# A two-block transformer on one core: the modulation dot products move to GpSimd, the third norm moves behind the projections, the first attention units run in pairs

## The reference

```
def memory_attention(q_mem, mem, mem_norm, w_mem_kv):      # first attention units: 4 heads of 64, 256 keys
    kv = rmsnorm(mem, mem_norm) @ w_mem_kv
    p = softmax(q k^T / 8);  o = p v

def first_block(x, mem, ...):
    ... layer a, layer b ...
    return rmsnorm(x, final_norm)

def _layer(x, c, ..., norm_g, w_ada, b_ada, w_in, ...):    # the third stage
    mod = c @ w_ada + b_ada                                # c: 1024 values, w_ada: 1024 x 3072
    shift, scale, gate = split(mod, 3)
    h = rmsnorm(x, norm_g) * (1 + scale) + shift
    proj = h @ w_in                                        # 1024 x 4096
    sb_q, sb_k, sb_v, sb_g, df_q, df_k, df_v, df_g = split(proj)
    ... stick-breaking attention (8 heads), differential attention (4 heads) ...
    return x + gate * (concat(sb_out, df_out) @ w_out)
```

## Time and profile before

| | us |
|---|---|
| median of 3 runs | 1594.12 (1592.28 to 1594.25) |
| profiled execution, its time | 1589.25 |
| its span | 1587.4 |
| TensorE busy | 1510.7 (95%) |
| VectorE busy | 931.4 (59%) |
| ScalarE busy | 671.4 (42%) |
| GpSimd busy | 110.5 (7%) |
| 24 loads of w_ada, issue to landing, median | 5.3 |

### The profile page before, as it was taken

The page is one execution under the profiler, slowest core; times in us unless marked ns, Lnnn a source line. Parts: engine busy times, 40 slices in busy tenths (PEclk is TensorE's granted clock), DMA queues, the critical chain, the costliest instruction groups (busy, mean ns, idle before and its releaser), DMA issues.

```text
span 1587.4 us, 20131 instructions
## 1 busy us (share of the span) xinstructions
PE 1510.7 (95%) x7120; PEld 1169.9 (74%) x7120; DVE 931.4 (59%) x1361; ACT 671.4 (42%) x1083; POOL 110.5 (7%) x127
## 2 busy tenths in 40 slices
PE   5988999999999999999989999999999799999998
PEld 4866677888888887766668888888887466667767
DVE  6668667777774335645445777777343644445662
ACT  6533344444443223434344444444222345555561
POOL 1269300000000000000000000000000010000000
PEclk9999999999999999999999999999999899999999
DMA  6544122223223222111112223223322111111221
GB/s 230 178 166 172 41 80 90 96 94 102 95 97 109 92 86 80 54 54 54 49 44 94 93 94 105 92 92 112 104 92 76 62 54 53 55 64 56 67 93 53
DMA packets 38146, 141.85 MB, mean 89 GB/s; under 512 B 4356, under 2 KB 4612, under 8 KB 38088
## 3 DMA queue, kind: packets, MB, share of 16 engines
q1 hardware_dynamic: 36936, 138.98, 25.8%
q10 hardware_dynamic: 1152, 2.10, 0.3%
HBM read 138.97 MB, written 2.10 MB: 89 GB/s over the span
## 4 chain that ended last, share of the span: by engine, by line
PE 83%; DVE 8%; ACT 5%; issue 2%; POOL 1%; DMA 1%; SPq 0%; ACTq 0%; DVEq 0%
PE ps L329 17%; PE ps L330 17%; PE ps L331 17%; PE ps L345 7%; PE ps L347 6%; PE ps L346 6%; DVE wl L263 2%; PE ps L510 2%; PE ps L580 1%; DVE rbc L426 1%; ACT wh L257 1%; PE ps L568 1%; PE ps L1796 1%; POOL aw L800 1%; PE ps L1786 1%
## 5 line engine op out<-in xcount | busy, mean ns | idle before, releaser
L257 ACT CAST wh<-raw 128x1024 fp32r<-128x1024 f32 (+1 forms) x213 | 234.0, 1099 | 312.1 <-PE ps L331 259.3
L263 DVE TENSOR_TENSOR wl<-raw,wh 128x1024 fp32r<-128x1024 f32 (+1 forms) x213 | 275.3, 1292 | 134.9 <-ACT wh L257 134.6
L329 PE MATMUL ps<-xh,wh 128*128 128x512 f32 x728 | 286.0, 393 | 9.7 <-DVE xl L1402 8.0
L330 PE MATMUL ps<-xl,wh 128*128 128x512 f32 x728 | 284.0, 390 | 0.0
L331 PE MATMUL ps<-xh,wl 128*128 128x512 f32 x728 | 283.9, 390 | 0.0
L345 PE MATMUL ps<-xh,wh 128*128 128x512 f32 x448 | 193.0, 431 | 2.5 <-DVE wl L263 2.5
L347 PE MATMUL ps<-xh,wl 128*128 128x512 f32 x448 | 177.8, 397 | 0.0
L346 PE MATMUL ps<-xl,wh 128*128 128x512 f32 x448 | 177.2, 396 | 0.0
L329 PEld LDWEIGHTS ps<-xh,wh 128*128 128x128 f32 x728 | 136.9, 188 | 43.6 <-issue 8.6
L331 PEld LDWEIGHTS ps<-xh,wl 128*128 128x128 f32 x728 | 137.1, 188 | 28.8
L330 PEld LDWEIGHTS ps<-xl,wh 128*128 128x128 f32 x728 | 137.1, 188 | 28.4 <-issue 0.5
(11 more groups left out here) (264 smaller groups left out, 2178.2 us busy)
## 6 DMA issues: line engine op xcount, KB each, us to landing
raw<-w_a_f SPq DMA_DIRECT2D x44, 512.0 KB, 3.2
raw<-w_b_f SPq DMA_DIRECT2D x44, 512.0 KB, 3.2
aw<-w_ada SPq DMA_DIRECT2D x24, 512.0 KB, 5.3
raw<-w_a_f SPq DMA_DIRECT2D x16, 704.0 KB, 4.1
raw<-w_b_f SPq DMA_DIRECT2D x16, 704.0 KB, 4.1
raw<-w_b_pair SPq DMA_DIRECT2D x18, 512.0 KB, 3.2
raw<-w_sb SPq DMA_DIRECT2D x16, 512.0 KB, 3.2
raw<-w_df SPq DMA_DIRECT2D x16, 512.0 KB, 3.2
```

The costliest lines, as they stand in the source:

```text
L257: nc.scalar.copy(wh[:, s, :width], raw[:, s, :width]).then_inc(w_hi, 1)
L263: nc.vector.tensor_tensor(wl[:, s, :width], raw[:, s, :width], wh[:, s, :width].bitcast(F32), ALU.subtract).then_inc(w_lo, 1)
L329: nc.tensor.matmul(dst, a, h(k), start=(k == 0), stop=False)
L330: nc.tensor.matmul(dst, a, l(k), start=False, stop=False)
```

## The change

1. The modulation no longer uses VectorE or TensorE. GpSimd loads, through its own queue, one tile of 128 rows of the transposed `w_ada` at a time (128x1024, 512 KB) into one buffer `rowt`, multiplies it by `vec`, a copy of `c_2` on every partition, and halves it ten times by additions until one column is left (`dot`). 24 such dots follow the first attention units. `vec` takes the place of the first layer's memory keys and values, so GpSimd waits for these units to be done.
2. After the 24 dots GpSimd forms `mod` and writes 8 diagonal tiles of the shift. Behind the `gate` chunk TensorE turns them with two matmuls into a copy of the shift on every partition, which ScalarE copies to `vec`. Then GpSimd makes 32 more dots, with the rows of `w_in_2` (another 16 MB from HBM): `csh`, what the shift adds to each column of each projection.
3. The third stage's projections run on x times gain and scale, which is split during `b_f2`. The norm's factor is applied when a projection leaves its bank, and for l = 0 to 2 a second instruction adds the column of `csh`; the gate's column goes in as the bias of its Silu. The first sum of squares goes to TensorE behind the first chunk of `sb`, the second behind the second.
4. The first layer's units run through `two_pe`, `two_act` and `two_dve`, which take their buffers as parameters.
5. SP's loads of `w_ada` are gone.

```diff
@@ gpsimd
-            for m in range(24):
-                a = aw[m % 6]
-                pool.wait_ge(ada_prod, m + 1)
-                for i, w in enumerate((4 * P, 2 * P, P)):
-                    wait(pool, ada_sum, 3 * m + i if i else 0)
-                    nc.gpsimd.tensor_tensor(a[:, 0:w], a[:, 0:w], a[:, w:2 * w], ALU.add).then_inc(ada_sum, 1)
+            def dot(i, rows, dst):
+                wait(pool, dot_sum, 11 * i)
+                pool.dma_start(rowt[:, :], rows).then_inc(row_in, 16)
+                pool.wait_ge(row_in, 16 * i + 16)
+                nc.gpsimd.tensor_tensor(rowt[:, :], rowt[:, :], vec[:, :], ALU.mult).then_inc(dot_sum, 1)
+                for e in range(10):
+                    w = 512 >> e
+                    pool.wait_ge(dot_sum, 11 * i + e + 1)
+                    nc.gpsimd.tensor_tensor(rowt[:, 0:w] if w > 1 else dst, rowt[:, 0:w], rowt[:, w:2 * w],
+                                            ALU.add).then_inc(dot_sum, 1)
+            pool.wait_ge(att["ma"]["pv"], 16)
+            pool.dma_start(vec[:, :], t["c_rep"]).then_inc(vec_in, 16)
+            pool.wait_ge(vec_in, 16)
+            for n in range(24):
+                dot(n, tile_rows("w_ada_rows", n), mod[:, n:n + 1])
...
+            for k in range(KD):
+                nc.gpsimd.tensor_scalar(rowt[:, k * P:(k + 1) * P], ident, mod[:, k:k + 1], None, ALU.mult).then_inc(diag, 1)
+            pool.wait_ge(rep, 2)
+            for n in range(32):
+                dot(24 + n, tile_rows("w_c_rows", n), csh[:, n:n + 1])
@@ vector, b_f2 and the third stage's start
                     nxt()
+                    x_lo_part(dve, X0["sb"], k, l // 2, modcol(8, k), xh, xl, square=False)
                     add_square(k, l // 2)
+            dve.wait_ge(ada_mod, 4)
             rounds(dve, "b_f2", 4, 4, split_lo, body)
-            norm_factor(dve, 5, rbc[:, :])
-            for k in range(KD + 1):
...
+            dve.wait_ge(dot_sum, 11 * 56)
+            q_shift = csh[:, 0:16].rearrange("p (u l) -> p u l", l=4)[:, :, 1:2]
+            nc.vector.tensor_scalar(q_shift, q_shift, QSCALE, None, ALU.mult).then_inc(k_cast, 1)
...
+                if n == C0["sb"]:
+                    split(u, l)
+                    norm_factor(dve, 5, rbc[:, :])
                 dve.wait_ge(w_used, n + 1)
...
-                    nc.vector.tensor_copy(dst, src).then_inc(po_free, 1)
-                if u == 0:
+                    nc.vector.tensor_tensor(dst, src, rbc[:, :], ALU.mult).then_inc(po_free, 1)
+                if l < 3:
+                    dve.wait_ge(po_free, J0["sb"] + 4 * u + l + 1)
+                    nc.vector.tensor_scalar(dst, dst, csh[:, 4 * u + l:4 * u + l + 1], None, ALU.add).then_inc(l_pr, 1)
@@ tensor
-            def ada(n):
-                pe.wait_ge(ada_sum, 3 * n + 3)
...
-                mem_att(att["ma"], u, "a", qma, pa, pta, (mix_lo, 1) if u else (m_vn, 4), between_a)
+                two_pe(pe, att["ma"], u, pa, pta, ..., (mix_lo, 1) if u else (m_vn, 4), between_a)
...
             norm_sum(pe, X0["kv"] + 8, 3)
+            pe.wait_ge(diag, KD)
+            for h in range(2):
+                nc.tensor.matmul(lg[h][:, :], ones, rowt[:, h * S:(h + 1) * S], start=True, stop=True).then_inc(rep_ps, 1)
...
             job(pe, [(C0["sb"], C0["sb"], KD)], J0["sb"], J0["sb"], X, XL, ready=(x_lo, X0["sb"]))
+            pe.wait_ge(n_hs, 24)
+            nc.tensor.matmul(st[:, :], ones, acc2[:, :], start=True, stop=True).then_inc(s_sum, 1)
+            blocks(pe, "sb", 1, X, XL, 0, KD)
             pe.wait_ge(s_root, 6)
             nc.tensor.matmul(st[:, :], ones, acc[:, :], start=True, stop=True).then_inc(s_sum, 1)
```

More of the change, by code:

```diff
@@ L104, in build @@
         cw = {L: par[:, NROWS + 176 * i:NROWS + 176 * (i + 1)].rearrange("p (a n) -> p a n", a=2) for i, L in enumerate("ab")}
-        km = {L: sb("km" + L, [P, 2, MEM], F32) for L in "ab"}
-        vm = {L: sb("vm" + L, [P, 2, MEM], F32) for L in "ab"}
+        vec_at = next_byte[0]
+        km, vm = {}, {}
+        for L in "ab":
+            km[L], vm[L] = sb("km" + L, [P, 2, MEM], F32), sb("vm" + L, [P, 2, MEM], F32)
+        vec = sb("vec", [P, D], F32, vec_at)
+        rowt = sb("rowt", [P, D], F32)
+        csh = sb("csh", [P, 32], F32)
         sm = sb("sm", [P, 64], F32)
@@ L427, in norm_factor @@
             dve.wait_ge(s_r, k + 1)
-        def att_pe(pe, a, it, q, k, v, nk, bias, first=None, o_free=None):
-            def turned(s):
-                h, i = divmod(s, TT)
-                n = nk(i)
-                pe.wait_ge(a["norm"], 8 * it + s + 1)
-                wait(pe, a["copy"], 8 * it + s - 1)
-                for b in range(n // P):
-                    mm = nc.tensor.transpose(tb[s % 2][:, b * P:(b + 1) * P],
-                                             first[:, s % 2, b * P:(b + 1) * P], ident)
-                mm.then_inc(a["turn"], 1)
-            def values(s, pt):
-                h, i = divmod(s, TT)
-                if s == 0 and o_free is not None:
-                    wait(pe, *o_free)
-                pe.wait_ge(a["copy"], 8 * it + s + 1)
-                for b in range(nk(i) // P):
-                    mm = nc.tensor.matmul(ob[heads(h), i * P:(i + 1) * P], v(h, b), pt[:, s % 2, b * P:(b + 1) * P],
-                                          start=(b == 0), stop=(b == nk(i) // P - 1))
-                mm.then_inc(a["pv"], 1)
-            def logits(s):
-                h, i = divmod(s, TT)
-                n = nk(i)
-                wait(pe, a["exp"], 8 * it + s - 1)
-                dst = lg[s % 2][:, :n]
-                more = bias(h, i, n)
-                mm = nc.tensor.matmul(dst, q(h, i), k(h, n), start=True, stop=not more)
-                for e, (c, l, r) in enumerate(more):
-                    mm = nc.tensor.matmul(lg[s % 2][:, c:n], l, r, start=False, stop=(e == len(more) - 1))
-                mm.then_inc(a["logit"], 1)
-            return logits, turned, values
@@ L585, in two_pe, with two_act @@
             pe_pairs(logits, turned, values, between)
[L587 removed]
+        def two_act(act, a, it, p, pt, nk, behind):
             def exps(s):
@@ new lines, in _ @@
+            pool.wait_ge(ada_mod, 1)
+            nc.gpsimd.tensor_scalar(mod[:, 8:16], mod[:, 8:16], 1.0, None, ALU.add).then_inc(ada_mod, 1)
+            for e, g in enumerate(("norm_g_2", "final_norm")):
+                pool.wait_ge(ada_mod, 2 + e)
+                nc.gpsimd.tensor_tensor(mod[:, 8:16], mod[:, 8:16], par[:, ROWS[g]:ROWS[g] + 8], ALU.mult).then_inc(ada_mod, 1)
+            for k in range(KD):
+                nc.gpsimd.tensor_scalar(rowt[:, k * P:(k + 1) * P], ident, mod[:, k:k + 1], None, ALU.mult).then_inc(diag, 1)
@@ L1711, in _ @@
             ffn("b", X0["b_f1"], 4)
-            pe.wait_ge(n_hs, 24)
-            nc.tensor.matmul(st[:, :], ones, acc2[:, :], start=True, stop=True).then_inc(s_sum, 1)
             def turn_values(u):
@@ L1930, in layout @@
     gate[:, 0:12] = kv[:, 2 * TOKW:2 * TOKW + 12]
-    heads4 = [chunk(w2, u + (4, 0, 8, 12)[l] + 16 * (u // 4) - 4 * (u // 4)) for u in range(8) for l in range(4)]
+    order4 = [u + (4, 0, 8, 12)[l] + 16 * (u // 4) - 4 * (u // 4) for u in range(8) for l in range(4)]
+    heads4 = [chunk(w2, c) for c in order4]
     out = {
@@ L1946, in layout @@
         "w_c_out": pack(*(chunk(a["w_out_2"][0], j) for j in range(KD))),
-        "w_ada": pack(*(chunk(a["w_ada_2"][0], n) for n in range(24))),
+        "w_ada_rows": pack(a["w_ada_2"][0].T),
+        "w_c_rows": pack(*(w2.T[c * P:(c + 1) * P] for c in order4)),
+        "c_rep": np.ascontiguousarray(np.broadcast_to(a["c_2"].reshape(1, D), (P, D))),
     }
```

176 lines of the change are left out of this document (49 added, 127 removed), and 2 rows, old and new, of the table PAR_ROWS.

## The result

The changed kernel is slower: 1616.24 us, median of 4 runs (1612.57 to 1618.31), against 1593.2 (1592.09 to 1594.25); the ratio is 1.0154 [1.0136, 1.0173]. The prediction was 1563 us with a range up to 1590 and a chance of 0.11 for slower: wrong in sign. The profiled execution took 1612.57 us, 23.3 more than that of before.

The account below looks back on a forecast made before the run. TensorE was taken to set the time nearly everywhere. Gains of 50.9 us less costs of 20.5 gave net −30.4: 1558.9 from the profiled 1589.25, plus 4.9 for the runs' median, said as 1563 us; range 1543 to 1590.

Parts of the forecast that it names:

- the feed-forward's term: Two first feed-forward halves: GpSimd's dots delay VectorE's weight splits through the shared port; cost 8 us, bounds 0 and 42.
- the clump: A dot's GpSimd product of 1024 columns and addition of 512 together, 2.4 + 1.3 = 3.7 us.
- B: Rival: VectorE becomes the bound beside the dots; 1587 us at worst, 1578 in the middle; chance 0.21.
- A: Rival: port conflicts between GpSimd and VectorE cost next to nothing, 3 to 8 us; time near 1548 us; chance 0.20.
- C: Rival: dots take 20 to 24 us and come late for `gate` and third stage; 1694 us; chance 0.11.
- the prediction's own signs of being wrong: First layer gains under 24 us, TensorE's `wl` waits in f1 sum over 20 us, or `ones` by `rowt` waits.
- Gain 1: Layer a's `a_in`: taking the modulation out brings the first unit's logits from 109.76 to 101.1 us; gain 8.7 us.
- Gain 2: First layer's two attention units run in pairs, as in layer b; gains 15.0 and 9.6 us.
- Gain 3: Third norm, last `b_f2` addition to transposes of first values: 23.2 us for 40.80; gain 17.6, between 14 and 18.
- One dot: GpSimd's load, product and additions for one dot take 14.7 us, load 4.2 of it; bounds 10.4 and 24.
- The small terms: Costs outside the feed-forward: spatial gating 3 us, layer b's attention 5, third stage's column additions 2.

Follow-up runs that it names:

- Run 5: Changed kernel, in first feed-forward halves a dot only every second round, its product held until the second tap of the first chunk ends: 1579.31 us, 0.9925.
- run 9: Changed kernel with a full dot only every fourth round of the first feed-forward halves, those between over one column (incomplete result): 1547.83 us, 0.9715.
- run 11: Changed kernel with dots on VectorE as one 1024-column operation, done twice in each round of the first feed-forward halves: 1566.91 us, 0.9857.
- Run 7: Changed kernel where GpSimd makes only each dot's product and ScalarE sums the row: 1601.12 us, 0.9994 to the kernel before is not this run; its ratio is 1.0056.
- run 1: Changed kernel with the dots' arithmetic cut to one one-column instruction, loads and waits kept (incomplete result): 1538.05 us, 0.9663.
- run 2: Changed kernel whose dots keep only the 1024-column product, the 512-column addition and the last one-column addition: 1591.07 us, 0.9993.
- run 10: Kernel before, with the modulation's VectorE products and GpSimd additions over one column, first units unpaired: 1572.43 us, 0.989.

## Why the prediction was wrong

**The step that failed** is the feed-forward's term: "The tightest split ends at 405.12, and TensorE wants it near 407.5 ...: 2.3 us of room. When the clump meets that place, 1.4 us are lost. ... I take it for a quarter of them, and some small change: 8 us. Bounds 0 and 30 × 1.4 = 42." Measured are 74.7, above the bound. The number of dots was right (31 of them start in the two halves); two things were wrong.

- *The room was taken for each dot anew.* 2.3 us is a stock, used up once; what a round puts back is 0.5 to 0.6 us (runs 5, 9 and 11). The earlier trace rows had half of it: VectorE waits 1.15 us for TensorE and then 0.40 for `wh`. Run 5's row has the other half: when VectorE comes 1.15 us earlier, it waits 1.04 for `wh`, so of the 1.15 only 1.15 − 0.64 = 0.51 are won there. I had read instead that VectorE was busy 7.95 of 10.88 us and called the rest free. With a dot in each round the loss is 3.16 − 0.61 = 2.55 (measured 2.6), not 3.7 − 2.3 = 1.4.
- *The places were taken as random.* In `a_f1` dot and round keep step at 13.5 us: the clump meets the split in 18 of its rounds, 17 of them running, and in 7 of `b_f1`, where the step was lost: 25 splits for 31 dots, not a quarter. That the two fall into step because each waits for the other is an inference from the timelines; no run shows it by itself. (Run 7 keeps step as well, by an explicit wait.) So an average over phases was no estimate here.

**The rivals.** B named the right engine, and its first sentence has "some 4.6 (GpSimd's held time) = 13.5 of 10.88 us", the very round of the trace. The size is luck: it adds 7.95 + 1 + 4.6, and the trace has 10.27 of cycle + 3.16 of delay; the gaps were put too low and the held time, for which no row stood, too high. I then charged 1.4 a dot from the other reasoning instead of 13.5 − 10.88 = 2.6, and so wrote 1587 "at worst". With 2.6 in 30 rounds the term is 78 instead of 8, and the forecast's sum −30.4 + 70 = +39.6: the right sign, 16 us above the traces' 23.4, since the halves lost 3 less than that and the other stretches did better by 13. A fell (runs 1 and 2). C fell: a dot took 11 to 15.6 us, no wait at `ones` by `rowt`. Of the prediction's own signs of being wrong one came: the waits for `wl` in the halves sum to 56 us, over the 20.

**Gain 1 and Gain 2.** The sum of 33.3 held (34.3, or 31.6 from the first chunk of `a_in` on). By place the parts held too: ahead of the units 8.1 from the first chunk on for the 8.7, in the units 23.5 (74.1 to 50.6 us) for 24.6. By cause they didn't. In the units the pairs alone bring 4.7 us, and 16.2 once the modulation is light (66.8 us in run 10 against 50.6, the modulation's steps on TensorE in it). The modulation's arithmetic alone brings 7.3 in the units. It stood in their way: of the 7.4 us of the earlier trace rows, 2.6 lay there, and I had put them all into `a_in`.

**Gain 3.** From the last addition to the first values 23.7 us pass now instead of 40.80: 17.1 for the forecast's 17.6, with a granted clock of 1.00 for 0.83. The other 2.3 us of the table's 19.4 lie ahead of it: the rounds of `b_f2` take 15.11 us instead of 15.40, at a granted clock of 1.00 in both. Why is not shown.

**One dot.** 14.7 forecast with 4.2 for the load. It is 13.5 in the feed-forward: product 2.47 (mean of the run) for 2.4, load 3.7, the 0.6 of its issue in it. The estimate from the Trainium skill's rule for such a load (DMA: Bandwidth & Descriptors, "Anatomy of one DMA — SWDGE (gpsimd) path") was 3.2; the trace has 3.7, and the measurement decides.

**The small terms.** Gating 4.5 for 3, layer b's attention 1.7 for 5, third stage near nothing for 2. Scalings of `pb` with 256 columns take 576 ns for 354, and TensorE has no wait for them that shows.

**What stays open.** How the loss divides between the product and the 512-column addition outside the rounds shown; whether the dots on GpSimd would be free at a place of the round that lets the product end ahead of the split; what brings dot and round into step, and why `b_f1` loses it; why the rounds of `a_f1` recover at 10.27 and those of `b_f1` at 10.37; how the third norm does by itself.

## What to carry to other kernels

Before work is put beside a loop, measure how long a round of the helping engines takes when they run unhindered, waits for each other included, and compare it with the bound engine's round: the difference is all that a round can absorb, and the time by which a buffer is early is only a stock. Two loops that delay each other can stay in step for many rounds (17 running here), so price the worst place in each round, not only the mean. And work that is small enough for the waiting gap of a fast engine (1.3 us on VectorE here) is better put there than on an idle slow one (9.4 us on GpSimd), which here took up to 3.2 us from the fast one anyway; if it has to go there, cut it: pieces of 256 columns won back 57 of the 78 us that the arithmetic cost.
